# A two-layer hybrid decoder trunk: layer 1's modulation work as steps of its own ahead of the layer border, gate rows in buffers of their own, and quarter products at the largest recurrence level

## What is computed

```python
def hybrid_layer(x, c, ...):
    mod = silu(c) @ ada_w + ada_b                 # 1024 -> 3072, one row
    shift, scale, gate = split(mod, 3)
    h = rms_norm(x, norm_g) * (1 + scale) + shift
    proj = h @ w_in                               # 1024 -> 8008 columns
    ya = hgrn2_mixer(...) * silu(hg_g)            # gated linear recurrence, 4 heads of 128
    yb = dsa_mixer(...) * silu(at_g)              # indexer, top 128 keys, attention
    yc = s5_mixer(...) * silu(s5_g)               # diagonal state space, then a GLU
    merged = sum_n sigmoid(merge_g[n]) * (y[n] @ w_branch[n])
    return x + gate * (merged @ w_out)
```

## Time and profile before

| | |
|---|---|
| median of three runs | 1290.11 us (1287.20 to 1292.71) |
| profiled execution, its own time | 1287.9 us |
| its span, first to last instruction | 1286.1 us |
| PE busy | 1250.2 us, 97% of the span |
| DVE busy | 870.4 us, 68% |
| ACT busy, POOL busy | 516.5 us, 497.7 us |
| mean granted PE clock | 0.996 |

### The profile page before, as it was taken

How to read it: one execution, slowest core, us unless ns; L and a number is a source line. 1 busy time by engine, 2 the same in 40 slices (tenths; PEclk the granted TensorE clock), 3 DMA queues, 4 the chain that set the end, 5 groups by cost and what they waited for, 6 DMA issues and landing times.

```text
span 1286.1 us, 16449 instructions
## 1 busy us (share of the span) xinstructions
PE 1250.2 (97%) x6240; PEld 1007.7 (78%) x6240; DVE 870.4 (68%) x1364; ACT 516.5 (40%) x858; POOL 497.7 (39%) x344
## 2 busy tenths in 40 slices
PE   7899999999999999999989999999999999999998
PEld 4687788887778878888748767888787888888887
DVE  5777886976587856777478468879656888544242
ACT  5253323763444333333233532256544443433331
POOL 1253243343544333555315322422444434255551
PEclk9999999999999999999989999999999999999999
DMA  9442111132234325473444221212321432244322
GB/s 354 145 162 69 64 53 63 54 127 66 66 92 113 103 75 209 157 254 100 165 158 169 75 107 50 66 52 64 131 66 50 140 99 68 75 150 162 98 82 66
DMA packets 63439, 142.04 MB, mean 110 GB/s; under 512 B 29440, under 2 KB 31616, under 8 KB 62592
## 3 DMA queue, kind: packets, MB, share of 16 engines
q1 hardware_dynamic: 54016, 137.84, 32.8%
q10 hardware_dynamic: 9344, 3.15, 1.0%
HBM read 128.12 MB, written 10.49 MB: 108 GB/s over the span
## 4 chain that ended last, share of the span: by engine, by line
PE 86%; DVE 5%; ACT 3%; DMA 2%; issue 2%; SPq 1%; POOL 0%; ACTq 0%; DVEq 0%
PE bank L1687 22%; PE bank L1689 22%; PE bank L1688 22%; PE bank L1875 4%; DMA raw<-in_wfull 2%; PE bank L1836 2%; PE bank L1860 1%; PE bank L1846 1%; SPq L721 1%; PE bank L1945 1%; PE bank L1699 1%; PE bank L1959 1%; PE bank L1958 1%; DVE h_lo L1359 1%; PE bank L1711 1%
## 5 line engine op out<-in xcount | busy, mean ns | idle before, releaser
L766 POOL TENSOR_TENSOR w_lo<-raw,w_hi 128x512 fp32r<-128x512 f32 (+1 forms) x170 | 241.2, 1419 | 769.0 <-ACT w_hi L800 769.0
L1687 PE MATMUL bank<-h_hi,w_hi 128*128 128x512 f32 x896 | 363.0, 405 | 2.1 <-ACT arena L874 2.1
L1689 PE MATMUL bank<-h_hi,w_lo 128*128 128x512 f32 x896 | 349.5, 390 | 0.0
L1688 PE MATMUL bank<-h_lo,w_hi 128*128 128x512 f32 x896 | 348.8, 389 | 0.0
L800 ACT ACTIVATE w_hi<-raw 128x1024 fp32r<-128x1024 f32 (+2 forms) x170 | 178.4, 1052 | 266.3 <-PE bank L1689 205.7
L767 POOL TENSOR_TENSOR w_lo<-raw,w_hi 128x512 fp32r<-128x512 f32 (+2 forms) x170 | 264.0, 1553 | 0.0
L1687 PEld LDWEIGHTS bank<-h_hi,w_hi 128*128 128x128 f32 x896 | 168.3, 188 | 42.9 <-issue 8.3
L1688 PEld LDWEIGHTS bank<-h_lo,w_hi 128*128 128x128 f32 x896 | 168.4, 188 | 38.7 <-issue 5.3
L1689 PEld LDWEIGHTS bank<-h_hi,w_lo 128*128 128x128 f32 x896 | 168.1, 188 | 35.8
L1687 PE MATMUL bank<-w_hi,h_hi 128*128 128x512 f32 (+1 forms) x256 | 97.6, 381 | 8.1 <-DVE h_lo L1359 4.4
L1688 PE MATMUL bank<-w_lo,h_hi 128*128 128x512 f32 (+1 forms) x256 | 95.3, 372 | 0.0
(11 more groups left out here) (276 smaller groups left out, 1797.8 us busy)
## 6 DMA issues: line engine op xcount, KB each, us to landing
raw<-in_wfull SPq DMA_DIRECT2D x178, 512.0 KB, 3.6
arena<-in_wada SPq DMA_DIRECT2D x40, 512.0 KB, 6.7
x_scratch<-xm SPq DMA_DIRECT2D x2, 2048.0 KB, 8.4
arena<-x_scratch SPq DMA_DIRECT2D x2, 2048.0 KB, 9.5
arena<-in_x SPq DMA_DIRECT2D x4, 512.0 KB, 5.6
arena<-in_s5m SPq DMA_DIRECT2D x2, 1024.0 KB, 6.4
u_scratch<-arena ACTq DMA_DIRECT2D x4, 512.0 KB, 4.0
arena<-u_scratch SPq DMA_DIRECT2D x8, 256.0 KB, 3.3
```

The source lines that it names most:

```text
L766: nc.gpsimd.tensor_tensor(lo[:, :half], raw_chunk(n)[:, :half], hi[:, :half].bitcast(F32), ALU.subtract)
L1687: mm(out_, a_hi, b_hi, start=first, stop=False)
L1688: mm(out_, a_hi, b_lo, start=False, stop=False)
L1689: return mm(out_, a_lo, b_hi, start=False, stop=last)
```

## The change

It is made in five parts.

1. The modulation work gets step kinds of its own: `adl` for the load on SP, `ada` for DVE's sums, `adm` for PE's two products. Each is placed by hand in the list, and `tensor_order()` goes.
2. Layer 1's gate chunks leave the `raw` ring (170 chunks are left, all split). Step `gin` p loads two of them into `gate_home`, eight arena buffers that are free late in layer 0; its SP part waits for the third branch's `y_done`.
3. `adp` 0 to 2 now come ahead of `("mod", 1, 0)`; `adp` 3 and `adr` 0 stand behind the projection `iq`, `adr` 1 behind `kvi`'s first chunk; none is left in the indexer part.
4. At part 7 (m = 64) PE multiplies only the first 64 by the second 64 positions of a block, and DVE copies that quarter without a mask.
5. The steps of both layers are reordered in many places, among them the recurrence's and the loads `mtin` and `uin`.

```diff
+        fetches = [("adl", l, i) for i in range(len(todo))]
+        columns = [("adm", l, p) for p in range(len(todo) // 2)]
...
-        steps += tm("kvi", 0) + rope("iq0") + rope("iq1") + rope("ik") + tm("kvi", 1) + late("adr", 0) + tm("kvi", 2) + rope("kn")
-        steps += tr("iqT3") + idx(1, 3) + late("adp", 2) + idx(1, 4) + cm("hq", 0, 1) + idx(1, 5, 6, 7) + hg(0, 0)
-        steps += cm("hf", 1, 0) + rope("k") + idx(2, 0, 1) + late("adp", 3) + idx(2, 2) + hg(0, 1) + late("adr", 1) + top1(0) + tr("kT")
...
-        steps += top(1) + tm("q", 3) + rope("qn") + hg(1, 7) + top(2) + top1(12) + hg(0, 9) + top1(13, 14) + cm("hg", 0, 0) + hg(1, 8)
-        steps += hg(0, 10, 11) + cm("hg", 0, 1) + top1(15) + rope("qs") + hg(0, 12) + hg(1, 9) + gate("hg", 0, 0, 1)
-        steps += cm("hg", 1, 0) + hg(1, 10, 11) + rope("q0") + rope("q1") + hg(1, 12) + top(3, 4) + cm("hg", 1, 1) + top(5) + tr("qT0")
...
-        steps += load("mtin", 3, 0, 1) + cm("mg1", 2, 1) + tab(3, 2) + s5(2, 4) + load("ysave", 2) + load("yback", 2) + s5(3, 2) + tab(3, 3)
-        steps += cm("wb1", 2) + s5(3, 3) + gelu(0, 1) + gelu(1, 1) + gelu(2, 0, 1) + cm("mg1", 3, 0) + s5(3, 4) + load("ysave", 3)
...
-        steps += cm("wo", 3, 0) + cm("wo", 2, 1) + next_layer("hs", 1) + cm("wo", 3, 1) + more(1) + out_tiles(1, 0, 1) + more(5)
-        steps += next_layer("hs", 2) + next_layer("adp", 0) + next_layer("hs", 3) + next_layer("mod", 0) + next_layer("adp", 1)
...
+        steps += late("adp", 3) + late("adr", 0) + rope("iq0") + rope("iq1") + rope("ik") + tm("kvi", 0) + late("adr", 1)
...
+        steps += tm("q", 3) + hg(1, 7) + hg(0, 9) + hg(1, 8) + cm("hg", 0, 0) + top1(11) + rope("qn") + hg(0, 10) + top1(12) + hg(0, 11)
+        steps += cm("hg", 0, 1) + top1(13, 14) + top(2) + top1(15) + rope("qs") + hg(0, 12) + hg(1, 9) + gate("hg", 0, 0) + hg(1, 10)
+        steps += cm("hg", 1, 0) + rope("q0") + hg(1, 11) + rope("q1") + gate("hg", 0, 1) + cm("hg", 1, 1) + hg(1, 12) + top(3, 4, 5)
...
+        steps += cm("mg1", 2, 0) + s5(3, 1) + load("mtin", 3, 0) + cm("mg1", 2, 1) + tab(3, 2) + load("uin", 3) + s5(2, 4) + load("ysave", 2)
+        steps += load("yback", 2) + s5(3, 2) + load("mtin", 3, 1) + tab(3, 3) + cm("wb1", 2) + s5(3, 3) + gelu(0, 1) + gelu(2, 0) + gelu(1, 1)
...
+        steps += cm("wo", 3, 0) + cm("wo", 2, 1) + next_layer("hs", 1) + cm("wo", 3, 1) + rows(1) + next_layer("adp", 0) + more(1) + rows(1)
+        steps += out_tiles(1, 0, 1) + fetch(2) + more(2) + fetch(1) + more(4) + next_layer("hs", 2) + next_layer("adp", 1, 2) + rows(1)
+        steps += fetch(1) + rows(1) + fetch(1) + next_layer("hs", 3) + rows(1) + out_tiles(2, 0, 1) + out_tiles(3, 0, 1)
+        steps += next_layer("mod", 0)
...
+                if kind == "gin":
+
+                    p = step[2]
+                    sp.wait_ge(y_done, gate_no(l - 1, 2, 3) + 1)
...
+                            if m == P // 2:
+                                half = [a.rearrange("p (c t) -> p c t", c=NT)[0:P // 2, :, P // 2:]
+                                        for a in (sct[:, 2 * g + i], banks[i][:])]
+                                v.tensor_copy(*half).then_inc(read((step, i)), 1)
+                                return
...
+                                if part == len(LEVELS):
+                                    first, second = slice(c * P, c * P + P // 2), slice(c * P + P // 2, (c + 1) * P)
+                                    last = mm(dst[0:P // 2, second], hk[:, 2 * g + i, first], hq[:, 2 * g + i, second],
+                                              start=True, stop=True)
+                                    continue
```

More of the change, by code:

```diff
@@ L70, in schedule, with taken, fetch, rows @@
         todo += [("ada", l + 1, c) for c in range(16)] if l + 1 < DEPTH else []
-        if todo:
-            todo.insert(12, ("mod", l, 16))
-        def more(n):
-            out = []
-            while todo and (n or todo[0][0] == "mod"):
-                n -= todo[0][0] == "ada"
-                out.append(todo.pop(0))
-            return out
+        fetches = [("adl", l, i) for i in range(len(todo))]
+        columns = [("adm", l, p) for p in range(len(todo) // 2)]
+        def taken(from_, n):
+            out = from_[:n]
+            del from_[:n]
+            return out
+        def more(n):
+            return taken(todo, n)
+        def fetch(n):
+            return taken(fetches, n)
+        def rows(n):
+            return taken(columns, n)
+        def first_gates():
+            return [("mod", 0, 16)] if l == 0 else []
         def tm(name, *cs_):
@@ L184, in chunks_of @@
     kind = step[0]
-    if kind == "adp":
-        return [ada_chunk(step[1], 16 + 2 * step[2] + kh) for kh in range(2)]
     if kind == "tm":
@@ L218 @@
 ADA_AT = {step: i for i, step in enumerate(ADA)}
-ADA_LAG = 3
-ADA_AHEAD = 1
-def tensor_order():
-    order, owed = [], []
-    for step in STEPS:
-        if step[0] == "mod":
-            order += [entry[0] for entry in owed]
-            owed = []
-        if step[0] == "ada":
-            if ADA_AT[step] % 2:
-                owed.append([step, ADA_LAG])
-            continue
-        order.append(step)
-        if chunks_of(step):
-            for entry in owed:
-                entry[1] -= 1
-            while owed and owed[0][1] <= 0:
-                order.append(owed.pop(0)[0])
-    assert not owed
-    return order
 def ad0_chunks(b):
     return [ada_chunk(0, 2 * b + kh) for kh in range(2)] + [ada_chunk(0, 8 + 2 * b + kh) for kh in range(2)]
-CHUNKS = [(c, step[0] == "adp") for step in STEPS for c in chunks_of(step)]
-CHUNK_K = [c[3] for c, _ in CHUNKS]
-CHUNK_W = [sum(w for _, w in c[4]) for c, _ in CHUNKS]
+CHUNKS = [c for step in STEPS for c in chunks_of(step)]
+CHUNK_K = [c[3] for c in CHUNKS]
+CHUNK_W = [sum(w for _, w in c[4]) for c in CHUNKS]
+GATE_ROWS = [(l, p) for l in range(1, DEPTH) for p in range(4)]
 def first_chunks():
@@ L268, in done_after @@
     for step in STEPS:
-        if step[0] != "adp":
-            n += len(chunks_of(step))
+        n += len(chunks_of(step))
         done[step] = done[group_of(step)] = n
@@ L370 @@
 NPOW = CH + 1
-def split_of():
-    out, n = {}, 0
-    for i, (_, is_ada) in enumerate(CHUNKS):
-        if not is_ada:
-            out[i] = n
-            n += 1
-    return out
-SPLIT_NO = split_of()
-SPLIT_CHUNK = sorted(SPLIT_NO)
 def split_upto(step):
@@ L394, in split_upto @@
         return DONE[step] + 1
-    if step[0] == "hk" and step[1] or step[0] == "adp" and step[2] < 2 or step[0] == "hs" and step[2] > 1:
-        return DONE[step] + (step[0] == "hk" and step[2] > 0)
     near = FIRST[step] + len(chunks_of(step)) + RAW_SLOTS
-    return min(DONE[step] + (3 if step[0] in ("gelu", "s5", "s5t") else 2), sum(n < near for n in SPLIT_CHUNK))
+    return min(DONE[step] + (3 if step[0] in ("gelu", "s5", "s5t") else 2), near, len(CHUNKS))
 SHIFTS = (0, 1, 2, 3)
 WARM = 8
-ADP_NO = {n: i for i, n in enumerate(n for n in range(len(CHUNKS)) if n not in SPLIT_NO)}
 def program(nc, wfull, wada, x, cvec, pos, lblog, vecs, gains, s5v, s5m, consts, masks, out):
@@ L547, in program @@
         ad0_acc, adp_used = sem("ad0_acc"), sem("adp_used")
+        gate_in = [sem(f"gate{p}_in") for p in range(4)]
         shift_in = [sem(f"shift{b}_in") for b in range(4)]
```

116 lines of the change are left out of this document (59 added, 57 removed).

## The result

The changed kernel takes 1279.93 us (median of eleven executions; the kernel before, eleven: 1291.31): 0.8% faster, ratio 0.9920 with a 95% interval of 0.9904 to 0.9935. Forecast were 1280.3 us and "faster". A few executions of some kernels took far longer (one of the changed kernel's eleven 3242.79 us, one of the four of experiment 12 1593.44 us), and the ratios, ranges and clocks given here leave them out.

A forecast was written before the change was run, and what follows sets the result against it. PE was taken as the bound, busy 1250.2 of 1286.1 us. Terms -4.8 - 3.5 - 3.3 + 1.4 + 0.4 = -9.8 took 1287.9 to 1278.1; 2.2 more for the median gave 1280.3 us, range 1275 to 1287.

The forecast's parts named there:

- Border and layer 1's start: Layer border and start of layer 1: -3.5 - 0.8 - 1.4 + 0.9 = -4.8 us (ends -6 and 0).
- The walk: New border order timed from 647.6: `mod` at 666.4, `iq` at about 669.9, DVE waiting 2.6 us for the tenth `adm`.
- The clock's cost: Half clock on `iq` for some 4 to 5 us: up to 1.5 us; border and clock together taken as 0.9 late.
- the three gains that I had listed: `adp` 2 done while PE would wait (3.5 us), `kvi`'s wait at L881 (0.8), wait before first recurrence products at L903 (1.4).
- State space part 3: Four of eight `mtin` transfers moved, weight load 2.5 us earlier, PE's waits for DVE's states go: -3.5 us (ends 0, -3.7).
- `uin` 3 has its buffer long free: State space loads: step claiming the moved load of u has its buffer free; no cost was put on it.
- Quarter products: Recurrence part 7: 64 PE instructions at 0.06 us instead of 0.111, -3.3 us (ends 0 and -3.5).
- the rival's floor of 0.11: Part 7: a floor per instruction holds quarter products at 0.11 us, kernel at 1283.6; chance 0.15.
- 102 changes from split products to other work: Whole list: 102 changes from split products to float32 work instead of 98, about 0.1 us each: +0.4 us.
- Recurrence order: Part 8's transposes wait for DVE's product and score copies: +0.7 us a layer, +1.4 us in all (ends 0 and +4).
- DVE did not fall behind: Rival, recurrence: DVE falls behind; typically 3 us a layer, 1286, chance 0.12; kernel slower, chance 0.04.
- The border did not give nothing: Rival, border: tenth `adm` delays `mod`, collisions stay, clock falls on `iq`; term 0 instead of -4.8, 1285; chance 0.16.

The follow-up runs named there:

- experiment 12: Changed kernel with the load of u for j = 3 early and 3 and 7 idle products where PE stands at the border: 1274.18 us, ratio 0.9882.
- experiment 5: Changed kernel with 7 and 14 idle float32 products where PE stands at the border, around the last `adm`: 1285.34 us, ratio 0.9962.
- experiment 6: Changed kernel with the last seven `ada` steps spread between the output chunks, `adp` 0 to 2 behind `hs` steps: 1273.69 us, ratio 0.9884.
- Experiment 8: Kernel before with only the second half of the `mtin` transfers for j = 3 moved behind state space part 2: 1285.63 us, ratio 0.9967.
- experiment 2: Changed kernel with the load of u for j = 3 put back ahead of the first four `mtin` transfers: 1276.12 us, ratio 0.9881.
- experiment 1: Changed kernel with whole 128 by 128 products and masked DVE copies again in part 7: 1282.77 us, ratio 0.9932.
- experiment 3: Changed kernel with the tenth `adm` ahead of `adp` 2 at the border: 1281.08 us, ratio 0.9930.
- experiment 4: Changed kernel with the first `hg` chunk ahead of the recurrence's part 8 instead of behind it: 1282.86 us, ratio 0.9933.

## Why the prediction was right, point by point

**The total.** Forecast 1280.3, measured 1279.93. The sum of the terms was -9.8; the traces give -8.7 and the medians -11.4. That the total came so near is in part luck. The state space gave +0.4 us where -3.5 was forecast; the border gave 0.8 us more than its term, and the recurrence with its products 1.8 more (-3.3 against -3.3 + 1.4 + 0.4); and the median of before had moved up by 1.2 us from the three executions that the forecast started from.

**Border and layer 1's start, -4.8: measured -5.6.** The walk held almost to the tenth of a microsecond: `mod` at 666.2 (walk: 666.4), first `iq` product at 669.75 (669.9), DVE's wait for the tenth `adm` 1.92 (2.6, of which a 0.71 us wait for a load took the rest). The splitting no longer collides with the h chain: `h_lo` takes 1.41 us for two instead of 3.31. The clock's cost was mis-sized. It fell before `iq` began and stayed low for 5.9 us of it, half of which is lost: 2.9 us, where I had allowed up to 1.5. PE reaches the third chunk at 683.54 instead of 681.98, 1.6 us late, not 0.9. The Trainium skill (TensorE: Matmul & The Clock Gate, "What's actually happening") has the clock fall when the array had little to do; the trace agrees here, and experiments 5, 6 and 12 show that it is the standing: with idle work in its place, or with no stand, the clock stays up there, and every trace that keeps the two stands has the low stretch. What came back for it were the three gains that I had listed, `adp` 2, L881 and L903, together 4.2 us net of the 1.6; 1.4 us more came that I had not costed. Most of it is in layer 1's indexer, which has more products in a row in the new order: its 16 products of 64x256 take 2.7 us to the instructions behind them instead of 4.8, of which 1.4 is the L903 wait already counted, so 0.7 is left, and those of 64x384 take 0.3 us less.

**State space part 3, -3.5: the term that failed.** The step was "`uin` 3 has its buffer long free", at the end of the paragraph on this term: I costed the moved load at nothing because its buffer was free, and did not ask when its data are needed. It was issued at 462.3 and PE wanted it at 465.3. The waits for DVE's states did go, as predicted; in their place came, at part 2, 0.94 and 0.62 us for u, and in layer 0 3.4 us of low clock. Together the term gave +1.8 in layer 0 and -1.4 in layer 1. Experiment 8 gives -4.4 by the medians and -3.8 by the traces for the `mtin` half of the edit alone, experiment 2 -3.8 by the medians and -4.2 in layer 0's trace for undoing the u half.

**Quarter products, -3.3: right in mechanism, a little large.** The products start 0.058 us apart (0.06 predicted), the rival's floor of 0.11 is not there. What was mis-sized is the group: 1.08 us from the first product to what follows, not 0.96, so 0.62 to 0.71 a part instead of 0.82: -2.6. On top came something that I had called no bound, DVE's copy, 0.41 instead of 0.72 us; in the new order it shortens the wait of part 8. The recurrence and what stands around it gained 3.3 us by the two traces, 1.5 more than the quarter products and the wait below explain. Of this 0.5 is in the waits view, where part 11 waits for ACT's copies for 0.5 us in the changed kernel (L1902 for L916) and for 1.0 before (L1919 for L941). The place of the rest stays open. The list does have 102 changes from split products to other work instead of 98, as counted, but no run prices them.

**Recurrence order, +1.4: measured +0.8,** 0.42 us a layer, since I had worked it out with the copies at their old length; with them it would have been 1.18 a layer (experiment 1).

**The rivals.** DVE did not fall behind: no new wait of PE on DVE in the recurrence besides part 8's. The border did not give nothing, although the clock fell on `iq` as that rival had it. The quarter products did get cheaper, 0.058 us and not 0.11.

## What to carry to other kernels

When a step is moved, ask of each of its transfers when its data are wanted, not only when its buffer is free. When a wait ends a phase, look at what the awaited engine did before: here DVE stood for 19 us just ahead of the work that everybody then waited for, and the list had put it there. And a stand of PE costs its own length and, now and then, a stretch at half clock behind it (3.4 us lost here); where it can't be removed, idle products of the measured length kept the clock here, though no gain in the time is shown for them (experiment 12). Taking the stand away (experiment 6) is what paid.

## What the runs showed of the hardware

A stand of 0.94 us (at 465.1) was followed by a low stretch of 6.8 us that began at 467.5, and stands of 0.83, 0.91, 0.94 and 1.07 us at the same place in experiments 6, 5, 3 and 4 likewise (10.2 us in experiment 3), while 2.37 us at 475.8 in the kernel before was not, nor was 0.62 at 1096.4. So the length of a stand does not tell whether the clock falls, and executions of one kernel differ by it: the changed kernel's ran from 1278.8 to 1285.9 us, the two slowest with the lowest mean clock (0.989). The low stretch at 60 us, behind the 3.7 us stand for the first `h_lo`, is 3.4 us long in seven of the fourteen traces and 6.8 in the other seven, whatever the edit. Two traces can differ by over 1 us from that alone, so they are compared from one split product to another and not by their ends.

Products with 64 weight columns and 64 positions start 0.058 us apart, where one side alone at 64 or 16 gives 0.112 and 0.116: in these rows the longer side sets the distance. Their weight load is shown as 138 ns, between the 192 and 97 of the earlier trace rows:

```profile
L1855 PEld LDWEIGHTS bank<-arena 128*64 128x64 f32 x64 | 4.0, 138 | 1.4 <-issue 1.4
```
